# RWKV key values summed onto state values in PSUM, gate pieces in other places, and a front with squares on two engines

## The reference

```
sh1, sc1, g1, sh2, sc2, g2 = split(silu(c) @ w_ada + b_ada, 6)
ch1, cs1, ... = split(silu(c_ctx) @ w_ada + b_ada, 6)
h_ctx = modulate(rms_norm(ctx, norm_mix_pre), ch1, cs1)
out_ctx, s_ctx, kv_ctx = token_mixer(h_ctx, 0, ..., emit=False)
h_lat = modulate(rms_norm(x, norm_mix_pre), sh1, sc1)
out_lat, _, _ = token_mixer(h_lat, s_ctx, ..., emit=True)

# token_mixer
p = h @ w_in
y_rwkv, s_fin = rwkv_branch(p_rwkv, s0)
g_rwkv, g_mla = split(sigmoid(p_gate + gate_b), 2)
merged = g_rwkv * (y_rwkv @ w_rwkv_proj) + g_mla * (o @ w_mla_proj)

# one step of the RWKV scan, for 16 heads of 64 and two directions
sa = S @ (-kk_t)
S = S * w_t + sa (x) (kk_t * a_t) + v_t (x) k_t
y = S @ r_t
```

## Time and profile before

| | us |
|---|---|
| median of 3 runs (3970.56 to 3986.98) | 3984.3 |
| the profiled execution, its own time | 3969.43 |
| its span, first to last instruction | 3967.6 |
| TensorE busy | 3681.3 (93%) |
| VectorE busy | 1310.8 (33%) |
| ScalarE busy | 531.9 (13%) |
| mean granted TensorE clock | 0.949 |

### The profile page before, as it was taken

One profiled execution on the slowest core, in us unless ns is written; L12 is line 12 of the kernel. 1 busy time (PEld: TensorE's weight loads), 2 busy tenths in 40 slices (PEclk: granted clock), 3 DMA queues, 4 the chain that ended last, 5 costly groups with the idle time before them and its releaser, 6 DMA issues.

```text
span 3967.6 us, 43277 instructions
## 1 busy us (share of the span) xinstructions
PE 3681.3 (93%) x18578; PEld 2923.2 (74%) x18578; DVE 1310.8 (33%) x1922; ACT 531.9 (13%) x907; POOL 163.4 (4%) x166
## 2 busy tenths in 40 slices
PE   6999999986988879998999999999899979999979
PEld 3464555545877668887888888888788858888858
DVE  1289342225668420102312222000261261070260
ACT  1100001223434200110100000000101120101120
POOL 0020000000000100000000000000050000050000
PEclk9999989987888789999999999999899989999989
DMA  7889313102321244443444444444244403344303
GB/s 309 331 358 379 131 55 113 53 32 48 82 55 29 83 152 156 148 170 127 148 149 148 151 155 148 150 157 150 96 149 140 147 22 138 117 149 148 128 32 127
DMA packets 129225, 551.50 MB, mean 139 GB/s; under 512 B 57009, under 2 KB 59185, under 8 KB 66625
## 3 DMA queue, kind: packets, MB, share of 16 engines
q1 hardware_dynamic: 113872, 447.26, 32.2%
q10 hardware_dynamic: 15200, 101.99, 6.6%
HBM read 533.48 MB, written 15.73 MB: 138 GB/s over the span
## 4 chain that ended last, share of the span: by engine, by line
PE 60%; DVE 2%; ACT 1%; issue 1%; ACTq 0%; POOLq 0%; DVEq 0%
PE ps L429 57%; PE ps L2643 1%; PE ps L2404 0%; PE ps L2651 0%; PE ps L2399 0%; PE ps L459 0%; PE ps L2335 0%; DVE arena L2700 0%; ACT arena L2778 0%; PE ps L2385 0%; DVE arena L2856 0%; PE ps L2652 0%; DVE arena L2165 0%; DVE arena L2839 0%; DVE arena L2620 0%
## 5 line engine op out<-in xcount | busy, mean ns | idle before, releaser
L429 PE MATMUL ps<-arena,ring 128*128 128x256 f32 (+3 forms) x11392 | 2626.1, 393 | 64.7 <-issue 22.6
L429 PEld LDWEIGHTS ps<-arena,ring 128*128 128x128 f32 (+1 forms) x11392 | 2172.1, 191 | 515.3 <-issue 214.0
L718 DVE SCALAR_TENSOR_TENSOR arena<-arena,small 128x512 f32<-128x512 f32 x240 | 194.2, 809 | 22.5 <-DVE arena L718 9.2
L2148 DVE TENSOR_TENSOR arena<-ps,arena 128x1024 f32<-128x1024 f32 x12 | 14.3, 1220 | 396.9 <-ACT arena L2134 396.9
L2523 DVE SCALAR_TENSOR_TENSOR arena<-arena,col 128x255 f32<-128x255 f32 (+29 forms) x180 | 108.2, 601 | 6.4
L561 PE MATMUL ps<-arena 128*128 128x512 f32 (+1 forms) x224 | 91.7, 558 | 5.3 <-ACT arena L614 5.3
L2267 DVE TENSOR_TENSOR arena<-ps,arena 128x1024 f32<-128x1024 f32 x11 | 13.5, 1224 | 239.2 <-PE ps L429 239.0
L2531 POOL TENSOR_TENSOR arena<-arena 128x1024 f32<-128x1024 f32 x2 | 4.7, 2352 | 2034.2 <-ACT arena L2472 2034.2
L1839 DVE TENSOR_TENSOR arena<-arena 64x30 f32<-64x30 f32 (+14 forms) x240 | 83.8, 349 | 8.2
L2246 ACT ACT_TABLE_LOAD x11 | 14.1, 1283 | 535.1 <-DVE arena L2280 535.1
L561 PEld LDWEIGHTS ps<-arena 128*128 128x128 f32 x224 | 42.0, 196 | 55.5 <-issue 54.2
(11 more groups left out here) (399 smaller groups left out, 3059.4 us busy)
## 6 DMA issues: line engine op xcount, KB each, us to landing
ring<-in_weights SPq DMA_DIRECT2D x404, 1024.0 KB, 4.8
arena<-in_ada_late ACTq DMA_DIRECT2D x64, 1024.0 KB, 8.5
arena<-in_front ACTq DMA_DIRECT2D x8, 1024.0 KB, 9.9
arena<-in_gates SPq DMA_DIRECT2D x32, 256.0 KB, 3.7
arena<-in_x ACTq DMA_DIRECT2D x2, 2048.0 KB, 15.0
arena<-in_ctx ACTq DMA_DIRECT2D x1, 2048.0 KB, 12.4
keep_h<-arena ACTq DMA_DIRECT2D x1, 2048.0 KB, 7.5
keep_o<-arena ACTq DMA_DIRECT2D x1, 2048.0 KB, 7.3
```

The costliest lines, as they stand in the source:

```text
L429: mm = M.matmul(o, ring[:, slot, k, c0:c0 + w], rhs, start=(kc == 0), stop=(kc == ktiles * WK - 1))
L718: ins = V.scalar_tensor_tensor(part[:, b], late[:, s, k], c, part[:, b], ALU.mult, ALU.add)
```

## The change

1. The front: x is loaded before ctx, and both after only the first 258 columns of the constants (identity, ones, fold) and the columns; each has a semaphore of its own. VectorE squares x, ScalarE ctx; VectorE adds 16 chunks of squares to four, and TensorE sums four. The first group's columns come before the reciprocals and the scaling.
2. The w_in stage: four late loads before ScalarE's first eviction (not eight); later evictions after late tiles 18 and 44 (not 22 and 52).
3. The latents: the late vectors are summed over partitions as rows first (ones, 32 columns, four column groups), copied by ScalarE and VectorE, and turned to columns by 16 matmuls with four columns of the identity.
4. RWKV: key values are accumulated onto the state values in the same PSUM columns (`first_products`), ScalarE copies the sum to U0; the separate copy Gv and VectorE's addition are gone. The first values of x=1 come between the two 32 merges. Own products follow the key (and rate) products. Gate pieces: four of each job before the own products (`own`), copied by ScalarE ahead of `turn_inverse`, four at one spot after the first merge, two after the second, one before the chain. SP loads the second four behind the unpacking. Semaphores of the front are cleared and used again.

```diff
...
+            first = 2 * P + 2
             a.dma_start(craw, A['c']).then_inc(c_in.sem, c_in.up(a, 16))
-            for dst, src in ((view(TMP + 4096, 4096), A['ctx']), (view(TMP, 4096), A['x']),
-                             (con[:], A['constants']), (col[:], A['columns'])):
-                a.dma_start(dst, src).then_inc(loaded.sem, loaded.up(a, 16))
-            for dst, src in ((col2[:], A['columns_2']), (dtw[:], A['dt_w'])):
+            a.dma_start(con[:, 0:first], A['constants'][:, 0:first]).then_inc(con_in.sem, con_in.up(a, 16))
+            a.dma_start(col[:], A['columns']).then_inc(con_in.sem, con_in.up(a, 16))
+            a.dma_start(view(TMP, 4096), A['x']).then_inc(x_in.sem, x_in.up(a, 16))
+            a.dma_start(view(TMP + 4096, 4096), A['ctx']).then_inc(ctx_in.sem, ctx_in.up(a, 16))
+            for dst, src in ((con[:, first:], A['constants'][:, first:]), (col2[:], A['columns_2']), (dtw[:], A['dt_w'])):
...
+            def norm_sum(q):
+                p.wait_ge(con_in.sem, 32)
+                p.wait_ge(sq_sum.sem, 2 - q)
+                for c in range(4):
+                    mm = M.matmul(ps[:, 5 + q, 0:T], C('ones'), xsq[q][:, c], start=(c == 0), stop=(c == 3))
+                mm.then_inc(norm_mm.sem, 1)
...
                 if g == 0:
-                    p.wait_ge(loaded.sem, 4 * 16)
-                    for q in range(2):
-                        norm_of[q][0](p)
+                    norm_sum(1)
                 fold(g)
+                if g == 0:
...
+            a.wait_ge(ctx_in.sem, 16)
+            for c in range(0, DC, 4):
+                S.activation(xsq[0][:, c:c + 4], xin[0][:, c:c + 4], ACT.Square).then_inc(ctx_sq.sem, 1)
...
-            for q in range(2):
-                norm_of[q][1](a, squares=False)
+            for q in (1, 0):
+                a.wait_ge(norm_var.sem, 2 - q)
+                S.activation(rs[:, q], rs[:, q], ACT.Sqrt).then_inc(norm_root.sem, 1)
...
+            def add_squares(q):
+                a = xsq[q]
+                V.tensor_tensor(a[:, 0:4], a[:, 0:4], a[:, 4:8], ALU.add).then_inc(dve_step.sem, dve_step.up(v))
+                step(V.tensor_tensor(a[:, 8:12], a[:, 8:12], a[:, 12:16], ALU.add))
+                V.tensor_tensor(a[:, 0:4], a[:, 0:4], a[:, 8:12], ALU.add).then_inc(sq_sum.sem, 1)
+                v.wait_ge(sq_sum.sem, 2 - q)
...
+            for c in range(0, DC, 4):
+                x = xin[1][:, c:c + 4]
+                V.tensor_tensor(xsq[1][:, c:c + 4], x, x, ALU.mult).then_inc(dve_step.sem, dve_step.up(v))
+            v.wait_ge(dve_step.sem, dve_step.now(v))
+            add_squares(1)
+            v.wait_ge(ctx_sq.sem, 4)
+            add_squares(0)
+            v.wait_ge(con_in.sem, 32)
...
                 v.wait_ge(dve_step.sem, dve_step.now(v))
+            norm_variance(1)
+            scales(0)
+            norm_variance(0)
+            for q in (1, 0):
+                v.wait_ge(norm_root.sem, 2 - q)
+                step(V.reciprocal(rs[:, q], rs[:, q]))
+            scale(0)
+            for j in range(4):
+                if j > 0:
+                    scales(j)
                 columns(2 * j + 1, 4 * j)
                 v.sem_inc(coef_ready.sem, 1)
...
-        LATE_AT = (8, 22, 52)
+        LATE_AT = (8, 18, 44)
...
+        def late_rows(p):
+
+            p.wait_ge(late_summed.sem, late_summed.due(p, 4 * LATE))
+            for b in range(LATE // 4):
+                q = 32 * (b % 4)
+                mm = M.matmul(ps[q:q + 32, 4 + b // 4, :], C('ones')[:, 0:32], part[:, b], start=True, stop=True,
+                              tile_position=(0, q))
+            mm.then_inc(late_row_mm.sem, 1)
...
         def late_columns(p):
 
-            p.wait_ge(late_summed.sem, late_summed.due(p, 4 * LATE))
-            for n in range(LATE):
-                mm = M.matmul(ps[:, 4, n:n + 1], part[:, n // 4, n % 4 * P:(n % 4 + 1) * P], C('ones')[:, 0:1],
-                              start=True, stop=True)
+            p.wait_ge(late_row_in.sem, 2)
+            for g in range(4):
+                for s in range(4):
+                    mm = M.matmul(ps[:, 4, (4 * g + s) * 4:(4 * g + s) * 4 + 4], late_row[:, g, s * P:(s + 1) * P],
+                                  C('ident')[:, 0:P:32], start=True, stop=True)
             mm.then_inc(late_mm.sem, late_mm.up(p))
 
+        def late_rows_in(eng, copy, g):
+
+            eng.wait_ge(late_row_mm.sem, 1)
+            copy(late_row[:, g:g + 2], ps[:, 4 + g:6 + g, :]).then_inc(late_row_in.sem, 1)
...
-            late_loads(a, 0, LATE_AT[0])
+            late_loads(a, 0, LATE_SLOTS)
             evict(kv[:, 0:4, :], ps[:, 0:4, :])
-            late_loads(a, LATE_AT[0], LATE_AT[1])
+            late_loads(a, LATE_SLOTS, LATE_AT[1])
...
+            late_rows(p)
...
+        STEPS, LATER = ("z5", "x5", "x5", "fin"), ("fin", "fin", "u", "u")
+        GATE_GROUPS = [(n, *g) for n in range(0, 4) for g in ((4, ("own",) * 4, "own"), (4, STEPS, "fin"))]
...
+            def gates_behind(n):
+
+                if n < 4:
+                    for i in gates_by(n, "fin"):
+                        load_gates(i)
+                    for i in gates_by(n, "own"):
+                        store_gates(i)
 
...
-            def key_values(n):
-                emit = n >= 4
-                for x in range(2):
-                    p.wait_ge(ev['mr_in'], mr_count(n, 4 if emit else x + 1))
-                    p.wait_ge(ev['tok_in'], 4 * n + 2)
-                    for h in range(8):
-                        mm = M.matmul(ps[:, (4 if emit else 6) + x, h * 64:(h + 1) * 64], MR[:, x, h, 0],
-                                      vtok(n, x, h), start=True, stop=True)
-                    mm.then_inc(ev['g_mm'], 1)
...
-            def state_values(n, x):
+            def first_products(n, x):
 
                 s, hf, q, i, b = job(n)
-                if x == 0 and n >= 4:
-                    p.wait_ge(ev['tr_in'], 2 * (n - 4) + 2)
-                elif x == 0:
-                    p.wait_ge(ev['mr_in'], mr_count(n, 2))
+                if x == 0:
+                    p.wait_ge(ev['mr_in'], mr_count(n, 4 if n >= 4 else 2))
+                    if n >= 4:
+                        p.wait_ge(ev['tr_in'], 2 * (n - 4) + 2)
                 t, st = slice(x * P, x * P + P), St[:, direction(n, x)]
                 for c in range(HF):
-                    for e in (0, 64):
-                        mm = M.matmul(ps[:, 2 * x + e // 64, c * 64:(c + 1) * 64], AR[e:e + 64, b, c, 0, t],
-                                      st[e:e + 64, hf * HF + c], start=True, stop=True)
+                    o = [ps[:, 2 * x + e, c * 64:(c + 1) * 64] for e in range(2)]
+                    for e in range(2):
+                        M.matmul(o[e], AR[64 * e:64 * e + 64, b, c, 0, t], st[64 * e:64 * e + 64, hf * HF + c],
+                                 start=True, stop=False)
+                    for e in range(2):
+                        mm = M.matmul(o[e], MR[:, x, 4 * e + c, 0], vtok(n, x, 4 * e + c), start=False, stop=True)
...
                 if more:
                     p.wait_ge(ev['dec_in'], n + 2)
-                key_values(n)
-                if more:
-                    p.wait_ge(ev['g_in'], 2 * n + 2)
+                    gate_pieces(n, "own")
+                    if n >= 4:
+                        p.wait_ge(ev['mr_in'], mr_count(n, 4))
+                    elif gates_by(n, "own"):
+                        p.wait_ge(gate_out.sem, gates_by(n, "own")[-1] + 1)
                     own_products(n + 1)
-                state_values(n, 0)
+                first_products(n, 0)
                 state_reads(n, 0)
                 merge_32_first(n)
-                gate_pieces(n, MIDST[0])
-                state_values(n, 1)
+                gate_pieces(n, "z5")
+                first_products(n, 1)
                 merge_32_second(n)
-                gate_pieces(n, MIDST[1])
+                gate_pieces(n, "x5")
                 state_reads(n, 1)
+                gate_pieces(n, "m64")
                 merge_64(n)
-                gate_pieces(n, MIDST[3])
+                gate_pieces(n, "fin")
...
-            def key_values(n):
-                for x in range(2):
-                    a.wait_ge(ev['g_mm'], 2 * n + x + 1)
-                    S.copy(Gv[:, x], ps[:, (4 if n >= 4 else 6) + x, :]).then_inc(ev['g_in'], 1)
+            def first_values(n, x):
+                a.wait_ge(ev['u0_mm'], 2 * n + x + 1)
+                S.copy(U0[:, x].rearrange("p (b t) -> p b t", b=2), ps[:, 2 * x:2 * x + 2, 0:256]).then_inc(ev['u0_in'], 1)
...
                     decays(n + 1)
+                    gate_copies(n, "own")
                 turn_inverse(n)
                 if more:
                     key_rates(n + 1)
-                key_values(n)
...
```

229 lines of the change are left out of this document (135 added, 94 removed).

## The result

The changed kernel took 4008.6 us (median of five runs, 4004.6 to 4019.5), the kernel before 3981.7 (3970.6 to 3987.0). The ratio is 1.0077, interval 1.0063 to 1.0091. 3948 was forecast, with 3920 to 3970 as the range; the sign was wrong too.

What follows compares the result with a forecast made beforehand. TensorE was taken as by far the busiest engine, time being won where it waits or runs at half clock. -19.5 - 4.8 - 11 + 8.4 = -26.9 gives 3942.5, raised to 3948 for run spread; range 3920 to 3970.

Steps and rivals of the forecast that it cites:

- part D: RWKV jobs 0 to 7: gate pieces and key values moved, +12.4 less 4 for the clock, net +8.4 us.
- I take 0: RWKV first products: 64-row and 128-row matmuls in turns cost nothing extra, from a range of 0 to +1.1 per half.
- the 4 us taken off for a clock that falls later in jobs 4 to 7: RWKV chains of jobs 4 to 7, at half clock before: a later clock fall saves 4 us, +12.4 becoming +8.4.
- the queue behind the gate copy: RWKV jobs 1 to 3: turned inverse and key rates wait behind ScalarE's gate copy; job 1's merge about 8.0 us later.
- R4: Jobs 0 to 3 from the own products: clock stays low to job end after the wait, +88, total +61, 4030; chance 0.03.
- The rule on idle stretches: RWKV own products: an idle stretch returns TensorE to half clock, so own and first products run at 1.2 GHz.
- R1: RWKV: shift in jobs 1 to 3 not taken back, mixed matmuls cost +9; RWKV +26, 3960 to 3966; chance 0.15.
- R2: RWKV jobs 4 to 7: clock holds, 20 more won, total -47, 3922 to 3928; chance 0.10.
- The front: Kernel start: overlapped loads and squares bring the second columns at 43 to 44 us, not 63.1; -19.5 us.
- Four tiles at 1.94 each end at 41: Front, second weight group: TensorE starts at about 33 and takes four half-clock tiles, giving second columns at 43.2 us.
- R3: Front: bound by the loads, -12 instead of -19.5, total -19, 3956; chance 0.07.
- w_in and latents: w_in stage: TensorE waits of 3.8 and 0.9 go, -4.8 us; latents: partition sums as rows, -11 (-9 to -12.5).

Runs made afterwards that it cites:

- e2: Changed kernel with each half's eight state-value matmuls grouped ahead of its eight key-value matmuls, not in turns: 3959.5 us, ratio 0.9963.
- e1: Kernel before with the new front, w_in stage and latents, RWKV edits undone: 3950.3 us, ratio 0.9933.
- e5: Changed kernel with grouped products, and ScalarE's gate copy moved behind the turned inverse and key rates: 3945.3 us, ratio 0.9926.
- e4: Changed kernel with the gate pieces of jobs 0 to 3 at their old places, number and banks: 4025.6 us, ratio 1.0119.
- e3: Changed kernel plus sixteen key-value matmuls repeated unread ahead of the own products in jobs 4 to 6: 3996.6 us, ratio 1.0053.
- e10: Gate copy late, grouped products, old key values in jobs 4 to 7; against that kernel (3924.3), first two side loads issued earlier: 3925.7 us, ratio 0.9868.

## Why the prediction was wrong

**The step that failed** is one clause of part D: "Whether 64-row and 128-row matmuls taken in turns overlap as well as 16 in a row, no row shows: between 0 and +1.1 per half, at most +9 over the path; I take 0". Three things in it are wrong. The size is the upper end: 0.86 a half at full clock and 1.15 at half (the table above, 7 changes against 1). The count is 16 halves, all on TensorE's path; eight of them ran wholly at half clock, so about 16 us. And its effect on the clock was not asked for: of the 45 to 49 us that the order alone gave back, the other 29 to 33 (a difference, not measured by itself) are merges, chains and products that ran at half clock, which with turns was the rule and without them the exception. The value 0 was taken since "the chain behind mixes two kinds in turns", but those two kinds both have 128 rows; the row count is what changes here.

The Trainium skill, TensorE: Matmul & The Clock Gate (Part 3: Packing small matmuls, The mechanism), says that a weight load is pulled ahead of matmuls in flight where it goes to other row groups or to the background weight buffer, and that it overlaps them only where the row groups differ. State values use the two 64-row halves by turns, a key value both, so by that rule a load waits at a change, and the trace agrees: 0.25 from load to load there. Two key values share all rows as well, and between them the trace shows 0.11, each load starting 0.056 after a matmul that is 0.275 long (its end is a modelled one). So the rule on row groups alone does not set a change apart, and it gives no price; it would have been a reason not to take 0, beside the one on idle gaps.

**The other steps of D** hold, but for one. With the products grouped, e2 lies 9.2 over e1 in the medians (12 by the ratios); 8.4 was forecast. In the traces its RWKV is 17.0 over before's and 6.4 over e1's, the same code. Its total, 3959.5, lies in the forecast's own range of 3930 to 3962. Job 0 of e2 became 5.9 shorter (4.7 forecast); in the changed kernel the wait before job 1's own products was 7.03 (6 to 8 forecast) and the first merge came 32.5 us into the job (33 forecast). That the queue behind the gate copy was the price in jobs 1 to 3 is shown by e5. The exception is the 4 us taken off for a clock that falls later in jobs 4 to 7: the changed kernel had 0.71, 0.65, 0.64 and 0.58 there, e2 0.79, 0.84, 0.84 and 0.64, before 0.84, 0.90, 0.84 and 0.70. No run shows that gain.

**The rivals.** R4 had the nearest total (4030) and the wrong place and cause. Half clock to the end of the job did come, but in jobs 4 to 7 and with matmuls in turns, not in jobs 0 to 3 from a wait: in jobs 1 to 3 of the changed kernel the clock was back within 7 us of each fall. That the dense pieces there bring it back fits e4, where it is at half through the first half of jobs 1 and 3, but is not shown apart. The rule on idle stretches that the prediction weighed (the Trainium skill, TensorE: Matmul & The Clock Gate, Why this matters for your kernels) fits the fall at 1229, which comes 0.7 us behind waits of 2.0 and 2.9, as in job 5 before; it does not fit the fall of e3, ahead of which TensorE had no wait for 17.6 us. R1's +9 for the turns was the same clause again, at half its size. R2 asked for the clock to hold in jobs 4 to 7 "since 2.2 us of dense matmuls now stand between the small ones"; the changed kernel takes them in turns, and in e2, where they are dense, the clock did not hold either (above).

**The front** gave 10.3 of the forecast 19.5. The second columns came at 53.1, 9.9 after the forecast 43.2. Half of it is the loads: x landed at 19.31 and ctx at 26.67 (15 and 22 estimated; the 3 us later for x that the prediction names were left out of its sum, since ctx was to hide them), so the second group's tiles start at 38.00 and not at 33:

```profile
19.40 4.63 DVE L660 TENSOR_TENSOR arena<-arena 128x1024 f32<-128x1024 f32 x4 [12.18 <-DMA arena<-in_x]
26.69 3.90 ACT L608 ACTIVATE arena<-arena 128x1024 f32<-128x1024 f32 x4 [20.02 <-DMA arena<-in_ctx]
```

The other half: "Four tiles at 1.94 each end at 41" leaves out how a tile is asked for:

```profile
38.00 2.78 PE L536 MATMUL ps<-ring,arena 128*32 128x512 f32 x24
48.40 1.93 PE L536 MATMUL ps<-ring,arena 128*32 128x512 f32 x8 [7.62 <-DMA ring<-in_weights]
```

```profile
39.08 2.04 SPq L359 DMA_DIRECT2D ring<-in_weights  x3
```

```profile
38.65 0.82 ACTq L500 DMA_DIRECT2D arena<-in_front  x2
```

Three tiles were in the ring and took 2.78, 3 less than counted. The fourth is issued when the group's first is used, 39.08, and two side loads of 1 MB were issued just ahead of it. The outcome is near R3's, and the loads' share of it was R3's cause. The sign was in the earlier trace rows: 1.46 of waiting for in_weights ahead of the fourth tile of the second group. Moving the side loads (e10) gave 4.5 back.

**w_in and latents** gave 9.2 and 12.9 against 4.8 and 11. Both waits of the earlier trace rows went whole (2.94 and 3.81; 0.9 had been allowed for the first); the remaining 2.4 are matmul rows that are shorter by that, from a cause that was not looked for. The front's error, these two and 3.0 in MLA, where nothing was forecast, cancel, which is luck. The 2547 us that the prediction calls the rest is a slip on which nothing rests: behind RWKV alone there are 2595 of the 3967.6.
